# State-space decays in a three-block kernel: eight per-head difference-and-clip instructions on GpSimd in place of one wide difference there and a clip on ScalarE

## The reference, cut to what matters

```
cum = jnp.cumsum(ai, axis=1)
seg = cum[:, :, None] - cum[:, None, :]
Lm  = jnp.exp(jnp.where(mask, seg, -jnp.inf))
cb  = jnp.einsum('btgn,bsgn->btsg', ci, bi)
y   = jnp.einsum('btsg,btsge,bsgep->btgep', cb, Lm, xi)
```

## Time and profile before

| | us |
|---|---|
| median of 3 runs | 4054.29 (4052.59 to 4057.67) |
| the profiled execution's own time | 4052.97 |
| its span (first to last instruction) | 4051.0 |
| state-space stages of the four groups, in the span | 3130.5 to 3399.4 |
| GpSimd busy over the whole span | 1408.1 (35%) |
| ScalarE busy over the whole span | 1209.9 (30%) |
| VectorE busy over the whole span | 2144.0 (53%) |
| TensorE busy over the whole span | 3401.6 (84%) |

### The profile page before, as it was taken

How to read it: one execution, slowest core, us unless ns; L and a number is a source line. 1 busy time by engine, 2 the same in 40 slices (tenths; PEclk the granted TensorE clock), 3 DMA queues, 4 the chain that set the end, 5 groups by cost and what they waited for, 6 DMA issues and landing times. The chain is left out here.

```text
span 4051.0 us, 44124 instructions
## 1 busy us (share of the span) xinstructions
PE 3401.6 (84%) x17568; PEld 2704.3 (67%) x17568; DVE 2144.0 (53%) x2514; ACT 1209.9 (30%) x1684; POOL 1408.1 (35%) x641
## 2 busy tenths in 40 slices
PE   7889988999888959988998875689964673789997
PEld 5668777888566749777886753478843352567885
DVE  5476667898554642347565556554353866422112
ACT  4223434232433212233233312333311221323222
POOL 3334343443332203343443321155401432333442
PEclk9999999999899979999999987799987776799999
DMA  3223354553322433444442222133312335222221
GB/s 114 78 68 125 122 165 142 199 204 115 123 75 81 122 72 99 143 140 145 146 142 93 79 73 82 64 106 117 104 40 92 98 114 178 94 83 81 97 91 65
DMA packets 229724, 442.70 MB, mean 109 GB/s; under 512 B 66144, under 2 KB 109856, under 8 KB 222992
## 3 DMA queue, kind: packets, MB, share of 16 engines
q1 hardware_dynamic: 224912, 431.50, 32.8%
q10 hardware_dynamic: 4608, 8.39, 0.5%
HBM read 387.44 MB, written 52.38 MB: 109 GB/s over the span
## 5 line engine op out<-in xcount | busy, mean ns | idle before, releaser
L356 POOL TENSOR_TENSOR second_feed_lo<-second_feed_raw,second_feed_hi 128x1024 fp32r<-128x1024 f32 (+3 forms) x182 | 407.2, 2238 | 788.9 <-ACT second_feed_hi L349 711.5
L356 POOL TENSOR_TENSOR first_feed_lo<-first_feed_raw,first_feed_hi 128x1024 fp32r<-128x1024 f32 (+4 forms) x182 | 396.9, 2185 | 599.1 <-ACT first_feed_hi L349 589.4
L356 POOL TENSOR_TENSOR third_in_feed_lo<-third_in_feed_raw,third_in_feed_hi 128x1024 fp32r<-128x1024 f32 (+1 forms) x81 | 198.2, 2450 | 467.6 <-ACT third_in_feed_hi L349 438.8
L273 PE MATMUL third_in_ps<-third_in_h_hi,third_in_feed_hi 128*128 128x512 f32 (+1 forms) x584 | 243.6, 417 | 72.0 <-DVE sctx_rows_out L936 25.8
L356 POOL TENSOR_TENSOR end_feed_lo<-end_feed_raw,end_feed_hi 128x1024 fp32r<-128x1024 f32 (+4 forms) x86 | 182.0, 2118 | 262.7 <-ACT end_feed_hi L349 262.7
L349 ACT ACTIVATE second_feed_hi<-second_feed_raw 128x1024 fp32r<-128x1024 f32 (+3 forms) x182 | 173.8, 956 | 210.9 <-PE ffn_low L275 70.8
L274 PE MATMUL third_in_ps<-third_in_h_lo,third_in_feed_hi 128*128 128x512 f32 (+1 forms) x584 | 235.7, 404 | 0.0
L275 PE MATMUL third_in_ps<-third_in_h_hi,third_in_feed_lo 128*128 128x512 f32 (+1 forms) x584 | 235.4, 403 | 0.0
L273 PE MATMUL mixer_acc<-first_h_hi,first_feed_hi 128*128 128x512 f32 x544 | 224.4, 412 | 12.7 <-DVE first_h_lo L428 7.4
L349 ACT ACTIVATE first_feed_hi<-first_feed_raw 128x1024 fp32r<-128x1024 f32 (+4 forms) x182 | 168.4, 929 | 193.5 <-PE mixer_acc L275 64.8
L518 DVE SCALAR_TENSOR_TENSOR ffn_ada_sum<-ffn_ada_w,cond,ffn_ada_sum 128x512 f32<-128x512 f32 x196 | 219.7, 1137 | 4.0
(11 more groups left out here) (775 smaller groups left out, 8857.0 us busy)
## 6 DMA issues: line engine op xcount, KB each, us to landing
second_feed_raw<-in_stream SPq DMA_DIRECT2D x130, 512.0 KB, 3.5
first_feed_raw<-in_stream SPq DMA_DIRECT2D x120, 512.0 KB, 3.3
ffn_ada_w<-in_w_ada SPq DMA_DIRECT2D x48, 1024.0 KB, 5.3
third_in_feed_raw<-in_stream SPq DMA_DIRECT2D x80, 512.0 KB, 3.8
end_feed_raw<-in_stream SPq DMA_DIRECT2D x52, 512.0 KB, 3.3
ssm_cum<-scratch_cum SPq DMA_DIRECT2D x32, 512.0 KB, 8.6
scratch_gates<-mixer_gate ACTq DMA_DIRECT2D x32, 256.0 KB, 2.2
mix_gin<-scratch_gates SPq DMA_DIRECT2D x32, 256.0 KB, 3.1
```

The costliest lines, as they stand in the source:

```text
L273: nc.tensor.matmul(out, w_hi, x_hi, start=start, stop=False)
L356: eng.tensor_tensor(self.lo[:, p % self.cut, :n], self.raw[:, p % self.deep, :n], self.hi[:, p % self.cut, :n].bitcast(F32), ALU.subtract) ...
```

## The change

Each difference (L3687) becomes eight `tensor_scalar` instructions on GpSimd, one per head: each reads 128 x 128 values of `cum`, subtracts the head's per-partition value of `cum_tok` and takes the minimum with 0.0. Only the last of the eight signals. The sign of the difference is the other way round, so the exponential needs no negative scale. The clip on ScalarE goes, with the semaphore between clip and exponential. Nothing is moved to another stage or queue; loads, buffers and waits on `cum` stay.

```diff
     pool.wait_ge(sems["cum_loaded"][c % 2], 64 * g + 32 * (c // 2 + 1))
-    by = cum_tok[:, c, 32 * d + 8 * g:32 * d + 8 * g + 8].unsqueeze(2).broadcast_to([P, 8, P])
-    nc.gpsimd.tensor_tensor(s["seg"][:, n % 4], by, s["cum"][:, c % 2, d], ALU.subtract
-                            ).then_inc(sems["diffed"], 1)
+    for h in range(8):
+        at = 32 * d + 8 * g + h
+        last = nc.gpsimd.tensor_scalar(s["seg"][:, n % 4, h], s["cum"][:, c % 2, d, h], cum_tok[:, c, at:at + 1], 0.0,
+                                       ALU.subtract, ALU.min)
+    last.then_inc(sems["diffed"], 1)
...
     act.wait_ge(sems["diffed"], 8 * g + n + 1)
-    nc.scalar.activation(seg, seg, ACT.Relu).then_inc(sems["clipped"], 1)
-    act.wait_ge(sems["clipped"], 8 * g + n + 1)
-    nc.scalar.activation(seg, seg, ACT.Exp, scale=-1.0).then_inc(sems["exped"], 1)
+    nc.scalar.activation(seg, seg, ACT.Exp).then_inc(sems["exped"], 1)
...
-        sems = {n: o.sem(n) for n in ("inputs_loaded", "diffed", "clipped", "exped", "y_stored")}
+        sems = {n: o.sem(n) for n in ("inputs_loaded", "diffed", "exped", "y_stored")}
```

## The result

The changed kernel takes 4148.35 us (median of 4 runs, 4144.67 to 4152.35) where the kernel before took 4053.44: a ratio of 1.0233, interval 1.0215 to 1.0250, or some 94 us more. The forecast was 4054 with a range of 4040 to 4078.

What follows compares the result with a forecast made beforehand. VectorE's state chain was taken to end sprep, TensorE's products after masks n = 4 and 5 sout. Per group +1.6 - 1.6 = 0, times four 0; 4052.97 + 0 = 4053.0, plus 1.3 for the median: 4054, range 4040 to 4078.

Steps and rivals of the forecast that it cites:

- the price s of one small instruction: GpSimd's start-to-start time per 128x128 tensor_scalar: 0.35 us taken, the affine select plus one more read; lower bound 0.25.
- upper bound: Highest price of one small GpSimd instruction: 0.46 us, from 0.10 fixed, two reads of 0.09 and 0.23, less 0.05.
- The reading of the Trainium skill: Against the change: a read command costs some 102 cycles, estimated 85 ns, without overlap; 8 x 2 reads replace 2.
- 3160.3 + 32 x 0.69: End of sprep's first group on ScalarE, forecast as 3160.3 + 32 s; with 0.35, 3171.5, or +1.6 us.
- the mask n = 7: VectorE mask in sout, first group: forecast to end at 3198.7, wanted at 3199.9, so still covered.
- GpSimd becomes the bound: Rival: small instructions of 0.40 us or more make sprep's last exponential late; 4077 at 0.46, 4116 at 0.60; chance 0.31.
- The order of what ends last: Sprep's end: VectorE's last addition before the change, ScalarE's exponential after it, near 41 us instead of 39.5.
- the clip matters only as latency: ScalarE is not scarce, having stood idle 145.6 us waiting for differences; its clips take 1052 ns each.
- The lock: Of a VectorE instruction with two SBUF inputs and a GpSimd one, the later waits for the whole of the earlier.
- The change does not let VectorE in: Rival: short GpSimd instructions in a row keep the port, sprep's VectorE chain ends some 10 us later per group, 4094; chance 0.03.
- VectorE's gain is hidden: Sprep: VectorE's chain gets faster, its first L3813 ending 1.4 us earlier, but GpSimd and ScalarE are late next.
- the cover: Sprep: the four differences were covered by VectorE's chain with 2.4 us to spare, which 32 small instructions eat.

## Why the prediction was wrong

The failed step is "the price s of one small instruction": forecast 0.35, with an upper bound of 0.46, measured 0.69. Of its terms one failed, the elements. The forecast has 0.11 us for 128 of them, and 0.23 for all else (0.10 fixed, 0.09 for a read, 0.09 for the operand, less 0.05); measured are 0.43 and 0.26, with the operand right (0.09 forecast, 0.085 measured). The second arithmetic step, 0.11 of the 0.69 and contained in these two, had no term at all. The element rate came from memset and affine select (0.9 ns), or at most from tensor_tensor (1.8 ns, with its fixed part), and tensor_scalar needs 3.3. The upper bound rested on the belief that an instruction with one streamed input could not be dearer per element than one with two; no row bore that out, and the range was cut by it.

The reading of the Trainium skill (GPSIMD Engine Reference) can now be set against a measurement. In the Trainium skill's table (Performance pitfalls for Q7 kernels) a read command costs some 102 cycles, 85 ns by my estimate; the operand costs 0.085 us here, the same number, though no run shows that the operand is such a read command. The Trainium skill's rule that one-input work runs at about line rate (Engine selection) did not hold here: 3.3 ns per element is slower than the two-input tensor_tensor of this same kernel, and the form with an immediate, which has one input only, is as slow (3.62 us for 128x1024), so here the measurement decides.

The other steps, taken with 0.69 in the place of 0.35, come out near. For sprep 3160.3 + 32 x 0.69 = 3182.4, +12.5 us against 10.3 to 11.3 measured: GpSimd was held up only some 0.1 us by most L3813, not 0.45. For sout the mask n = 7 would end at 3209.7, 8.2 late, against 10.8 to 12.8 measured; some 2 us of the rest is TensorE, which waits in between and runs its last 16 products at the lower clock (3.67 in place of half of 3.68). Together 83 us forecast by the corrected sum, 91 measured.

- "GpSimd becomes the bound" was the rival that happened, by its own mechanism and in both stages; it was priced to 0.60 and given 0.31.
- The order of what ends last was right: VectorE's chain before, ScalarE behind GpSimd after.
- That the clip matters only as latency was right: taken away alone it gives nothing in sprep and 8 us in sout.
- The lock was right for the wide tensor_tensor. "The change does not let VectorE in" did not happen with tensor_scalar (longest mask 1.23 us), but it did with small tensor_tensor, against which the row between two wide differences was no evidence.
- That VectorE's gain is hidden was right. Its size was not: 1.4 us were forecast, with the products bounding each step at 2.05. The chain of the changed kernel got 3.6 shorter, its last products being two in 1.10 us, and with the cover off sprep gained 3.4 to 4.4.

## What to carry to other kernels

Fusing two steps saves one engine's latency, but it is paid at the element rate of the fused form on the engine that gets it. If no row shows that form on that engine, the bound from other operations is no bound: keep the range open upward, and multiply it by the number of instructions that it stands before (256 here: the 0.34 us by which each was dearer than forecast came to 91 us, 27 for each 0.1). A difference with a per-partition operand and a clip in one is cheap on VectorE (0.20 us per 128x128) and ScalarE (0.29), dear on GpSimd (0.69), and there it is the elements that cost, not the operand.

## What the runs showed of the hardware that was not expected

- GpSimd's tensor_scalar on f32 costs 3.3 ns per element with subtract and min, its tensor_tensor 1.7 (0.36 us for 128x128 and 1.86 for 128x1024, start to start) and its affine select 0.9, all on the same partitions and type.
- A wide tensor_tensor on GpSimd holds a VectorE instruction with two SBUF inputs until it ends; a tensor_scalar does not, not even a wide one: it held one issued 0.22 us behind its start by 0.74 us, and one issued 1.2 us behind it not at all.
- The small tensor_scalar instructions held L3813 by at most 0.14 us (0.83 for 0.69) and the masks not at all. VectorE in turn holds GpSimd up: the instruction behind a mask's start took 1.57 us in place of 0.71.
- Small tensor_tensor instructions held one mask of each group for 7.4 us, until their row ended; a wait for the completed last instruction of each eight ended that.
